# Retention products rebuilt around whole pairs of heads; the second norm's transposes kept on the chip; loads of the second and third tile group issued piece by piece into new homes

## The chip, the cores and the metric

One core of one Trainium2 chip runs the kernel. The metric is device microseconds, the median of the timed runs. Engines are named as the profile names them: PE (TensorE), DVE (VectorE), ACT (ScalarE), POOL (GpSimd), SP (the queue of loads and stores).

## The reference

One layer over 1024 prompt tokens and 8 x 16 sample tokens, 1152 in all (nine tiles of 128 tokens: `t` 0 to 7 are the prompt, tile 8, called `ST`, the samples). All in float32.

```
h = rms_norm(x, norm1_g); z = h @ w_in            # 8 retention heads, 8 fox heads, 64 wide each
retention per chunk: sc = (q k^T) * decay mask
                     o  = sc v + (q S) * q_dec;   S = S * s_dec + (k * k_dec)^T v
forgetting attention per head (softmax over all earlier tokens, cumulative log-forget bias)
x1 = x + concat(norm(ro) * silu(rg), norm(fo)) @ w_out
PEER: xn = rms_norm(x1, norm2_g); scores of 2 x 8 x 128 keys, top 16 of 16 x 16 pairs per head,
      act = gelu(sum(xn * u[e])); y = x1 + sum(g * act * v[e])        # 128 experts e per token
```

For each token PEER fetches 128 rows of 2048 numbers (`u` and `v` of one expert side by side), so a tile of 128 tokens needs 128 gathers of 128 rows of 8 KB.

## The kernel before, in words

Four phases follow one another: norm, projections of the retention keys and values, `phase_retention`, the fox projections of the first three tiles, and then `phase_tail`, which is most of the time.

**Retention.** Tiles are taken in `ORDER` = 0, 1, ST, 2, ..., 7. In one iteration PE makes the scores of the next tile (`scores`, in two halves: even heads at partitions 0 to 63, odd heads at 64 to 127), the eight gate products of this tile (`gate(t, k)`, 128x512 each, spread between the others), and the outputs: per head one product of the masked scores with the values (L683) and one of the queries with the state (L686, on 64 partitions). `up` (L694) is the update of the state. DVE masks scores, updates the state, and forms the gated output; for four tiles PE and DVE also make a piece of the sample tiles' state (L732). `outputs_sample` (L706, L710) is the sample tile, whose products over 64 rows are only 16 columns wide. `WARM` adds two bf16 products ahead of each gate run.

**Tail.** Nine tiles in three groups of three (`g`). Per gather POOL issues an indirect DMA into a ring of nine buffers; DVE makes the dot product of the fetched `u` with the token's `xn`, spread over partitions (`xrep`); for each four gathers ACT and DVE form weights, and PE adds the `v` halves into `yp` (`add_v`, eight products of 128x512, four at a time on 32 columns each), after which the buffers are free (`uv_free`) and POOL goes on. `replicate_x` and `spread_x` make `xrep` of the next tile near a tile's end; `finish` closes a tile. Everything else of a group (fox attention, `w_out`, second norm, keys, top-k: the "front") is dealt between these steps: `front_steps` lists the steps with what each waits for, and `deal` puts them at fixed places of each engine's program by estimated durations. An engine runs its program strictly in order. Gathers of a tile need that tile's experts, so the first three tiles' gathers follow the front of group 0, and the fronts of groups 1 and 2 run beside gathers.

The transposed `xn` of each tile is stored to the scratch `xts` (L1539) and loaded back one tile ahead (L1557) for `replicate_x`; `x1` is stored too (L1528) and loaded for the sum in `finish` (L1577).

Of the kernel before, what the change touches and what calls it, by code (L numbers as in the profile page):

```python
# [12 lines left out]
ALU = mybir.AluOpType  # L13
# [3 lines left out]
P = 128  # L17
# [15 lines left out]
def emit(nc, a):  # L33

    ctx = ExitStack()
    with ctx:
# [555 lines left out]
        def phase_retention(block, sem, ps):  # L592
# [15 lines left out]
            op_all = [ps(f"op{i}", [P, GW]) for i in range(2)]  # L608
            op = [b[:, 0:PAIRS * HD].rearrange("p (r e) -> p r e", r=PAIRS) for b in op_all]
# [12 lines left out]
            pool_step, gate_exp = sem("pool_step"), sem("gate_exp")  # L622
# [37 lines left out]
            def _(pe):  # L660
                def scores(t, half):
                    s = AT[t]
                    if s >= 1:
                        pe.wait_ge(mask_done, 2 * (s - 1) + half + 1)
                    for r in range(PAIRS):
                        b0 = 64 * half
                        last = nc.tensor.matmul(sc[half][:, r, :], kT[b0:b0 + 64, r, t * P:(t + 1) * P],
                                                qT[b0:b0 + 64, r, t * P:(t + 1) * P], start=True, stop=True)
                    last.then_inc(sc_done, 1)

                def outputs(t):
                    s = AT[t]
                    if t >= 1:
                        pe.wait_ge(oev, t)
                        pe.wait_ge(st_done, t)
                    if t == 2:
                        pe.wait_ge(oTm, 1)
                    for h in range(NH):
                        if h < 2:
                            pe.wait_ge(mask_done, 2 * s + h + 1)  # L680
                        b0, r = 64 * (h % 2), h // 2
                        o = op[h % 2][:, r, :]
                        last = nc.tensor.matmul(o, sT[:, s % 2, h % 2, r, :], vn[:, t, h * HD:(h + 1) * HD],  # L683
                                                start=True, stop=(t == 0))
# [3 lines left out]
                        if h == NH - 1:  # L688
                            last.then_inc(o_done, 1)
                        if s and h % 2:  # L690
                            gate(t, 2 + h // 2)
                    for h in range(NH):
# [7 lines left out]
                def outputs_sample():  # L700
# [3 lines left out]
                    for h in range(NH):  # L704
# [9 lines left out]
                        if h in (0, 1, 2, 4, 5, 6):  # L714
                            gate(ST, h + (1 if h < 3 else 0))
# [1772 lines left out]
```

## Time and profile before

| | |
|---|---|
| time, median of 3 runs | 3847.42 us (3836.97 to 3848.2) |
| the profiled execution's own time | 3865.37 us |
| its span | 3863.6 us |
| busy: PE, DVE, POOL, ACT | 2370.1, 2448.0, 1428.5, 473.8 us |
| moved by DMA in the span | 1357.89 MB, of them 1208.03 MB by gathers |
| retention begins, fox projections begin, first gather issued | 226, 427, 692 us |

The rows below come from that one execution, so sums are made against 3865.37 us. It is 17.95 us above the median of the three runs. Each float32 product of the code shows as two MATMUL records on PE.

### The profile page before, as it was taken

What the parts mean: (1) busy time and instruction counts of PE and PEld (TensorE: products, weight loads), DVE (VectorE), ACT (ScalarE), POOL (GpSimd) and SP (SyncE); (2) the same over time, 40 slices, a digit from 0 to 9 for tenths busy, and PEclk for the clock granted to TensorE, in tenths of its full rate; (3) what the DMA queues carried; (4) which work ended last, traced back from release to release, by engine and by line L of the source; (5) the groups of instructions that cost most, each with busy time, mean ns of one, the idle gap of its engine ahead of it and who ended that gap; (6) DMA issues with size and microseconds to landing.
All of it is one profiled execution on the core that took longest, in us unless ns stands there. A gap on an engine that the chain in (4) does not pass through costs nothing.

```text
span 3863.6 us, 34930 instructions
## 1 busy us (share of the span) xinstructions
PE 2370.1 (61%) x11957; PEld 970.8 (25%) x11957; DVE 2448.0 (63%) x6334; ACT 473.8 (12%) x1311; POOL 1428.5 (37%) x1275
## 2 busy tenths in 40 slices
PE   8999989778477566846547655684343334334333
PEld 4455445323133122314213311231010001001000
DVE  4225324989566556878966655788886555555555
ACT  2001132202022010102112200110111000000000
POOL 1001100265344443433444444434444444444443
PEclk9988999989688787967668877897666556566655
DMA  3010451899999999999999999999999999999998
GB/s 117 22 39 17 130 191 55 334 395 406 411 410 415 420 418 394 409 391 404 415 417 420 409 420 418 409 407 416 409 407 422 421 420 417 413 422 410 421 421 366
DMA packets 251073, 1357.89 MB, mean 351 GB/s; under 512 B 33792, under 2 KB 53064, under 8 KB 103440
## 3 DMA queue, kind: packets, MB, share of 16 engines
q0 software_dynamic: 165888, 1208.03, 75.8%
q1 hardware_dynamic: 84720, 147.04, 10.5%
q8 instruction: 95, 1.56, 0.2%
q14 instruction: 82, 0.67, 0.0%
q10 hardware_dynamic: 288, 0.59, 0.0%
HBM read 1325.22 MB, written 30.35 MB: 351 GB/s over the span
## 4 chain that ended last, share of the span: by engine, by line
DMA 36%; PE 20%; DVE 16%; POOL 8%; issue 6%; ACT 1%; another core or an unknown queue 0%; POOLq 0%; DVEq 0%; ACTq 0%
DMA M<-in_peer_uv,M 36%; PE yp L2067 12%; POOL M L1632 8%; DVE M L2352 6%; PE ab L2020 1%; PE ef L2055 1%; DVE exg L2369 1%; DVE strips L2374 1%; PE ab L1861 1%; PE c L1999 1%; PE d L1883 1%; DVE M L2119 1%; PE d L1999 1%; DVE gel L2361 1%; DVE M L2118 1%
## 5 line engine op out<-in xcount | busy, mean ns | idle before, releaser
L1632 POOL DMA_INDIRECT M<-in_peer_uv,M x1152 | 1321.8, 1147 | 1801.5 <-PE yp L2067 1445.0
L2352 DVE SCALAR_TENSOR_TENSOR M<-M 128x1024 f32<-128x1024 f32 x1152 | 1411.0, 1226 | 856.5 <-DMA M<-in_peer_uv,M 824.5
L2067 PE MATMUL yp<-M,strips 128*32 128x512 f32 x4608 | 898.5, 921 | 1279.4 <-DVE strips L2374 1253.8
L2067 PEld LDWEIGHTS yp<-M,strips 128*32 128x32 f32 x4608 | 159.2, 144 | 1888.4 <-DVE strips L2374 1490.5
L1813 ACT ACTIVATE gel<-gel 128x4 f32<-128x4 f32 x288 | 59.2, 205 | 2151.8 <-DVE gel L2363 2117.5
L2020 PE MATMUL ab<-M 128*128 128x512 f32 x576 | 264.9, 608 | 1.3 <-ACT M L1769 1.3
L426 PE MATMUL z<-M 128*128 128x512 f32 x432 | 190.1, 597 | 0.9 <-PEq L105 0.9
L2020 PEld LDWEIGHTS ab<-M 128*128 128x128 f32 x576 | 108.2, 196 | 137.6 <-issue 136.1
L1900 PE MATMUL ab<-M 128*128 128x512 f32 x288 | 130.6, 605 | 5.2 <-DVEq L2229 5.2
L867 POOL TENSOR_SCALAR small<-small 128x8 f32<-128x8 f32 x9 | 2.6, 285 | 331.7 <-DVE small L837 331.7
L426 PEld LDWEIGHTS z<-M 128*128 128x128 f32 x432 | 81.3, 191 | 97.5 <-issue 97.4
L2374 DVE SCALAR_TENSOR_TENSOR strips<-gel,exg 128x128 f32<-128x128 f32 x288 | 84.0, 292 | 32.9 <-ACT gel L1813 22.5
L2352 DVE DVE_READ_ACCUMULATOR M<-M 128x1 f32 x1152 | 95.0, 83 | 0.0
L2055 PE MATMUL ef<-ident,M 128*32 128x128 f32 x2304 | 86.7, 290 | 13.2 <-issue 11.9
L1873 PE MATMUL c<-ident,M 128*128 128x128 f32 x288 | 56.1, 308 | 61.1 <-ACT M L1666 60.4
L2246 DVE CUSTOM_DVE_ANT_0 M<-ab,M 128x896 f32<-128x896 f32 (+6 forms) x64 | 48.4, 756 | 70.6 <-PE ab L1862 59.3
L747 PE MATMUL z<-M 128*128 128x512 f32 x144 | 91.9, 738 | 0.8 <-DMA M<-in_w_in 0.8
L1861 PE MATMUL ab<-M 64*128 64x512 f32 (+3 forms) x192 | 87.9, 568 | 5.1 <-DVE mins L2246 5.1
L2369 DVE TENSOR_TENSOR exg<-e,gel 128x128 f32<-128x128 f32 x288 | 84.0, 292 | 10.0
L1883 PE MATMUL d<-M 128*64 128x128 f32 x576 | 89.1, 308 | 0.9 <-ACT M L1674 0.9
L2055 PEld LDWEIGHTS ef<-ident,M 128*32 128x32 f32 x2304 | 69.1, 117 | 39.1 <-issue 29.3
L1883 PEld LDWEIGHTS d<-M 128*64 128x64 f32 x576 | 72.5, 156 | 18.0 <-issue 16.2
(248 smaller groups left out, 2517.6 us busy)
## 6 DMA issues: line engine op xcount, KB each, us to landing
M<-in_peer_wq SPq DMA_DIRECT2D x12, 2048.0 KB, 28.5
M<-in_w_in SPq DMA_DIRECT2D x9, 2048.0 KB, 11.3
M<-in_peer_uv,M POOLq DMA_INDIRECT x1152
M<-in_w_out SPq DMA_DIRECT2D x24, 512.0 KB, 23.4
M<-in_x_prompt SPq DMA_DIRECT2D x16, 512.0 KB, 10.9
x_scratch<-M SPq DMA_DIRECT2D x9, 512.0 KB
xts_scratch<-M SPq DMA_DIRECT2D x9, 512.0 KB
M<-xts_scratch SPq DMA_DIRECT2D x9, 512.0 KB
```

What stands on the lines that cost most here:

```text
L426: last = nc.tensor.matmul(z[n % 3][:, :], hT[:, k, t * P:(t + 1) * P], wbuf[:, slot(gi), k, :], start=(k == 0), stop=(k == KC - 1))
L747: last = nc.tensor.matmul(z[s % 2][:, :], hT[:, k, t * P:(t + 1) * P], w_gate[k], start=(k == 0), stop=(k == KC - 1))
L1632: nc.gpsimd.indirect_dma_start(ring[n % NR], None, a["peer_uv"], bass.IndirectOffsetOnAxis(ap=idxH[:, t % 6, s // 4, s % 4:s % 4 + 1], axis=0)
L1861: nc.tensor.matmul(s[:, c:c + w], rows_q[b0:b0 + 64, r], rows_k[b0:b0 + 64, r, c:c + w], start=True, stop=c + w < width)
L1883: last = nc.tensor.matmul(Dk[b0:b0 + 64, 0:P], (vg if g else vn)[:, j, h * HD:(h + 1) * HD], pT[:, n % 2, j, :], start=(j == 0), stop=(j = ...
L1900: last = nc.tensor.matmul(half_ab[j % 2], hTl[i][:, k, :], pw[q % 2][:, k, :], start=(k == 0), stop=(k == KC - 1))
L2020: last = nc.tensor.matmul(half_ab[i % 2], xT[:, tt, k, :], wq(g, b)[:, k, :], start=(k == 0), stop=(k == KC - 1))
L2055: last = nc.tensor.matmul(EF[32 * b:32 * b + 32, half, k * P:(k + 1) * P], xTn[:, 4 * half + k, 32 * j:32 * j + 32], ident[:, :], start=Tr ...
L2067: last = nc.tensor.matmul(yp[32 * j:32 * j + 32, 512 * c:512 * c + 512], strips[:, n % 2, j, :], ring[(4 * n + j) % NR][:, D + 512 * c:D + ...
L2352: nc.vector.scalar_tensor_tensor(out=row, in0=row, scalar=1.0, in1=xrep[:, s % 4, :], op0=ALU.mult, op1=ALU.mult, accum_out=dots[:, t % 2, ...
L2369: link(nc.vector.tensor_tensor(exg[:, :, :], bc(e32[:, :].unsqueeze(1), [P, 4, 32]), bc(g[:, 3, :].unsqueeze(2), [P, 4, 32]), ALU.mult))
L2374: nc.vector.scalar_tensor_tensor(out=strips[:, n % 2], in0=bc(g[:, 2, :].unsqueeze(2), [P, 4, 32]), scalar=1.0, in1=exg[:, :, :], op0=ALU. ...
```

## The change

**Retention.** `scores` alternates the two halves head by head. The state is also written as a block-diagonal matrix `bd` (two heads per 128x128 block, zeroed once by POOL, its two diagonal parts written by two more DVE instructions per tile), and the eight state products on 64 partitions become four on 128, after the eight score products of the tile. The outputs of all heads lie in one bank per tile, and ACT moves them in one copy instead of two. Gate products 0 and 1 follow each other, and those of the sample tile all come after its outputs.

**Tail.** The scratch `xts` is gone: no store, no load. `x1` is loaded once per tile into the buffer that held the transposes (`load_x1`, `x1b`), DVE makes the normalised row again (`make_row`), PE spreads it by identity products, and PE adds `x1` into `yp` by eight identity products at the start of a tile, so `finish` is a copy. The loads of groups 1 and 2 are cut up: keys (`loadk`), the rest of the attention's data (`load`), `w_out` half by half (`wload`, `hload`), query weights (`qload`, `rload`) and keys, each issued when its new home is free. Planner costs change with them.

```diff
+                def scores(t):
                     for r in range(PAIRS):
+                        for half in range(2):
+                            b0 = 64 * half
+                            last = nc.tensor.matmul(sc[half][:, r, :], kT[b0:b0 + 64, r, t * P:(t + 1) * P],
+                                                    qT[b0:b0 + 64, r, t * P:(t + 1) * P], start=True, stop=True)
...
-                        if t:
-                            last = nc.tensor.matmul(o, qT[b0:b0 + 64, r, t * P:(t + 1) * P],
-                                                    st[b0:b0 + 64, r, :], start=False, stop=True)
...
+                        for r in range(PAIRS):
+                            last = nc.tensor.matmul(o[:, r * P:(r + 1) * P], qT[:, r, t * P:(t + 1) * P], bd[:, r, :],
+                                                    start=False, stop=(r == PAIRS - 1))
...
-                        if h in (0, 1, 2, 4, 5, 6):
-                            gate(ST, h + (1 if h < 3 else 0))
...
+                    whole = s == 0 or t == ST
...
+                    for b0 in (0, 64):
+                        nc.vector.tensor_tensor(bd[b0:b0 + 64, :, b0:b0 + 64], new[b0:b0 + 64], sd[b0:b0 + 64], ALU.mult)
+                    nc.vector.tensor_tensor(st, new, sd, ALU.mult).then_inc(st_done, 1)
...
-                add(rest, ("load", g), sp=(55.0 if g else 6.0, *routed))
                 if g:
-                    add(rest, ("loadq", g), sp=(40.0, *chosen))
+                    at = routed if nt < GT else [("sp", ("pturn", 0, 2 * LATE - 1)), ("pe", ("pmm", 0, 2 * LATE - 1, 1))]
+                    add(rest, ("loadk", g), sp=(25.0, *at))
+                add(rest, ("load", g), sp=(40.0 if g else 6.0, *routed))
...
-                        sp.dma_start(a["xts"][t], xT[:, arg[0]].rearrange("p k n -> p (k n)")).then_inc(xT_out, 16)
...
+                def load_x1(t):
+                    sp.wait_ge(x1_out, 16 * GT * (t // GT + 1))
+                    if t >= 1:
+                        sp.wait_ge(x1b_used, t)
+                    sp.dma_start(x1b, a["x1"][t]).then_inc(x1b_in, 16)
...
-                        for k in range(4):
-                            for b in range(4):
-                                last = nc.tensor.matmul(EF[32 * b:32 * b + 32, half, k * P:(k + 1) * P],
-                                                        xTn[:, 4 * half + k, 32 * j:32 * j + 32], ident[:, :],
-                                                        start=True, stop=True)
+                        for b in range(4):
+                            last = nc.tensor.matmul(EF[32 * b:32 * b + 32, half, :], ident[:, 32 * j:32 * j + 32],
+                                                    xb[:, 512 * half:512 * half + 512], start=True, stop=True)
...
+                    if k == 0:
+                        pe.wait_ge(x1b_in, 16 * (t + 1))
+                        for c in range(2):
+                            for j in range(4):
+                                last = nc.tensor.matmul(yp[32 * j:32 * j + 32, 512 * c:512 * c + 512], ident[:, 32 * j:32 * j + 32],
+                                                        x1b[:, 512 * c:512 * c + 512], start=True, stop=False)
+                        last.then_inc(x1b_used, 1)
...
-                    nc.vector.tensor_tensor(xb, yp[:, :], xb, ALU.add).then_inc(y_out, 1)
+                    if t + 1 < TILES:
+                        dve.wait_ge(rep_mm, 8 * t + 16)
+                    else:
+                        dve.wait_ge(out_done, 16 * t)
+                    nc.vector.tensor_copy(xb, yp[:, :]).then_inc(y_out, 1)
+
+                def make_row(t):
+                    dve.wait_ge(x1b_in, 16 * (t + 1))
+                    dve.wait_ge(xrs, t + 1)
+                    if t >= 2:
+                        dve.wait_ge(out_done, 16 * (t - 1))
+                    nc.vector.scalar_tensor_tensor(out=xb, in0=x1b, scalar=rst[:, t:t + 1], in1=grow[:, :],
+                                                   op0=ALU.mult, op1=ALU.mult).then_inc(row_done, 1)
```

PE before, in retention, the iteration of tile 1 from its start (`sc` scores, `z` gate, `op` outputs of two heads):

```order
L667 MATMUL sc_3<-M 128x128 x4
L745 MATMUL z_3<-identb 128x512 x2
L747 MATMUL z_3<-M 128x512
L667 MATMUL sc_3<-M 128x128 x4
L747 MATMUL z_3<-M 128x512
L683 MATMUL op_3<-M 128x64
L686 MATMUL op_3<-M 128x64
L683 MATMUL op_3<-M 128x64
L686 MATMUL op_3<-M 128x64
L747 MATMUL z_3<-M 128x512
```

The same place of the changed kernel, up to the end of the tile's outputs:

```order
L668 MATMUL sc_3<-M 128x128 x8
L747 MATMUL z_3<-identb 128x512 x2
L749 MATMUL z_3<-M 128x512 x2
L681 MATMUL op_3<-M 128x64 x2
L749 MATMUL z_3<-M 128x512
L681 MATMUL op_3<-M 128x64 x2
...
L749 MATMUL z_3<-M 128x512
L691 MATMUL op_3<-M 128x128 x4
L698 MATMUL up<-M 64x64 x8
```

The scores stand together, the alternation of L683 and L686 is gone, and four wide products (L691) follow the last head.

PE before, from the scores ahead of the sample tile to the first of its eight heads (`opT`) and the gate product behind it:

```order
L667 MATMUL sc_3<-M 128x128 x8
L745 MATMUL z_3<-identb 128x512 x2
L747 MATMUL z_3<-M 128x512
L706 MATMUL opT<-M 64x128
L710 MATMUL opT<-M 64x16 x8
L747 MATMUL z_3<-M 128x512
```

The end of the sample tile in the changed kernel, and the start of the next iteration:

```order
L710 MATMUL opT<-M 64x128
L714 MATMUL opT<-M 64x16 x8
L747 MATMUL z_3<-identb 128x512 x2
L749 MATMUL z_3<-M 128x512 x8
L723 MATMUL up<-ident,M 128x128 x4
L668 MATMUL sc_3<-M 128x128 x8
```

All eight gate products of the sample tile now stand in a row behind its narrow products.

DVE of the changed kernel in the top-k work ahead of the first gather (L2200 and L2208 are the choice of experts of tile 0; before, nothing stood between L2127 and L2169, which are L2158 and L2200 here):

```order
L2154 MAX M<-M 128x8 x4
L2158 MAX_INDEX M<-M 128x8 x4
L2424 SCALAR_TENSOR_TENSOR M<-M,dec 128x1024
L2200 MAX_INDEX M<-M 128x8 x4
L2208 CAST M<-M 128x64
```

`make_row(0)` (L2424) has moved in between, and PE's `replicate_x` of tile 0 waits for it.

## Rows read from the trace of the kernel before

**Rows 1.** The page: mean busy share of the DMA engines, in 40 equal slices, tenths.

```profile
DMA  3010451899999999999999999999999999999998
```

**Rows 2.** Windows by phase: length, busy us (instructions) of each engine, granted clock, DMA share, GB/s.

```profile
226.00:427.00 201.00, 198.63 (x886) 114.97 (x887) 91.87 (x112) 18.85 (x40) 17.48 (x19) 0.83 0.15 44
427.00:692.00 265.00, 243.48 (x1068) 123.99 (x1068) 96.59 (x345) 69.61 (x173) 21.30 (x28) 0.97 0.36 124
692.00:3864.00 3172.00, 1721.82 (x9431) 632.71 (x9429) 2193.40 (x5768) 353.96 (x1045) 1380.03 (x1206) 0.73 1.00 411
```

**Rows 3.** Waits: us in total, times, longest us.

```profile
POOL M L1632 <- ACT M L1680: 76.3, 3, 75.7
```

**Rows 4.** DMA from 692 us on: packets; issues with KB each.

```profile
DMA packets 209074, 1302.72 MB, mean 411 GB/s; under 512 B 21024, under 2 KB 29280, under 8 KB 61472
...
M<-xts_scratch SPq DMA_DIRECT2D x7, 512.0 KB
...
xts_scratch<-M SPq DMA_DIRECT2D x6, 512.0 KB
```

**Rows 5.** Timeline of PE, tile 4 of retention: start, us, what, records.

```profile
343.73 1.16 PE L667 MATMUL sc<-M 64*128 64x128 f32 x8
...
348.26 0.33 PE L683 MATMUL op<-M 128*128 128x64 f32 x2
348.52 0.43 PE L686 MATMUL op<-M 64*128 64x64 f32 x2
...
349.61 1.13 PE L747 MATMUL z<-M 128*128 128x512 f32 x2
...
357.60 0.69 PE L694 MATMUL up<-M 128*64 128x64 f32 x16
...
361.33 1.16 PE L667 MATMUL sc<-M 64*128 64x128 f32 x8
```

**Rows 6.** Timeline of PE, runs of one kind: tile 0's outputs, a projection.

```profile
231.07 3.67 PE L683 MATMUL op<-M 128*128 128x64 f32 x16
...
448.98 7.03 PE L426 MATMUL z<-M 128*128 128x512 f32 x16
```

**Rows 7.** Timeline of PE, sample tile and tile 2.

```profile
263.07 1.71 PE L667 MATMUL sc<-M 64*128 64x128 f32 x16
...
266.46 1.10 PE L710 MATMUL opT<-M 64*64 64x16 f32 x16
...
272.57 1.89 PE L710 MATMUL opT<-M 64*64 64x16 f32 x16
...
297.44 2.07 PE L667 MATMUL sc<-M 64*128 64x128 f32 x8
...
326.13 1.16 PE L667 MATMUL sc<-M 64*128 64x128 f32 x8
```

**Rows 8.** Windows of 10 us in retention, columns as in Rows 2.

```profile
230.00:240.00 10.00, 9.19 (x43) 6.78 (x41) 2.49 (x4) 1.28 (x3) 1.84 (x2) 0.50 0.95 240
240.00:250.00 10.00, 10.00 (x32) 4.84 (x31) 2.56 (x2) 0.60 (x1) 0.00 (x0) 0.87 0.02 3
```

**Rows 9.** Timeline of DVE, tile 4 of retention: first and last of 13 rows.

```profile
358.33 0.42 DVE L814 TENSOR_TENSOR M<-up,M 128x256 f32<-128x256 f32 x1 [4.19 <-PE up L694]
...
370.45 1.29 DVE L804 TENSOR_TENSOR M<-sc,causal 128x512 f32<-128x512 f32 x2 [0.21 <-DVE M L846]
```

**Rows 10.** Timeline of PE and POOL ahead of the first gather.

```profile
657.40 7.32 PE L2055 MATMUL ef<-ident,M 128*32 128x128 f32 x256
...
713.09 0.94 POOL L1632 DMA_INDIRECT M<-in_peer_uv,M  x1 [9.28 <-PE yp L2067]
```

**Rows 11.** Timeline at the end of tile 7.

```profile
3535.13 1.90 PE L2067 MATMUL yp<-M,strips 128*32 128x512 f32 x16
...
3539.27 0.34 SPq L1571 DMA_DIRECT2D out_y_prompt<-M  x1
...
3541.76 3.64 PE L2067 MATMUL yp<-M,strips 128*32 128x512 f32 x16 [4.73 <-DVE strips L2374]
```

More of the change, by code:

```diff
@@ L750, in gate @@
                         last.then_inc(z_done, 1)
-                for half in range(2):
-                    scores(0, half)
+                scores(0)
                 for s, t in enumerate(ORDER):
-                    for half in range(2):
-                        if s + 1 < TILES:
-                            scores(ORDER[s + 1], half)
-                        if t == ST:
-                            if half:
-                                gate(t, 0)
-                        elif s:
-                            gate(t, half)
+                    whole = s == 0 or t == ST
+                    if s + 1 < TILES:
+                        scores(ORDER[s + 1])
+                    if not whole:
+                        gate(t, 0)
+                        gate(t, 1)
                     if t == ST:
@@ L768, in _ @@
                         state_sample(PIECE[t])
-                    for k in range(KC - 1 if s else 0, KC):
+                    for k in range(0 if whole else KC - 1, KC):
                         gate(t, k)
@@ L863, in _ @@
             def _(pool):
+                nc.gpsimd.memset(bd[:, :, :], 0.0).then_inc(bd_set, 1)
                 for s in range(TILES):
@@ L880, in _ @@
                         act.wait_ge(o_done, t + 1)
-                        for par in range(2):
-                            last = nc.scalar.copy(
-                                mixo[:, t, 0:GW].rearrange("p (r q e) -> p q r e", q=2, e=HD)[:, par], op[par])
-                        last.then_inc(oev, 1)
+                        nc.scalar.copy(mixo[:, t, 0:GW], op[t % 2][:, :]).then_inc(oev, 1)
                         act.wait_ge(oev, t + 1)
@@ L906, in emit @@
         NR = 9
+        ROW = P - 20
         def tiles_of(g):
@@ L996, in values @@
                 t, nt = FOX[n][2], len(tiles_of(g))
+                wait = [("sp", ("load", g))] if g and n == FIRST[g] else []
                 add(rest, ("foxv", g, n),
-                    pe=(0.1 + 0.33 * (t + 1), ("act", ("foxq" if t >= 4 else "foxp", g, n)),
+                    pe=(0.1 + 0.33 * (t + 1), ("act", ("foxq" if t >= 4 else "foxp", g, n)), *wait,
                         *bank("D", "act", ("foxv", g, n))),
@@ L1044, in front_steps @@
                 full = ("dve", ("fout", g, PAIRS - 1))
-                add(rest, ("hload", g), sp=(50.0 if g else 12.0, full))
+                add(rest, ("hload", g), sp=(30.0 if g else 12.0, full))
                 for i in range(GT):
@@ L1189, in work_ready @@
                 if e == "dve":
+                    if i % P == ROW and i // P + 1 < TILES and ("sp", ("hadd", (i // P + 1) // GT, GT - 1)) not in done:
+                        return None
                     return None if i >= len(landed) or summing() else landed[i]
@@ L2393, in _ @@
                             finish(t - 1)
+                        if s == ROW and t + 1 < TILES:
+                            make_row(t + 1)
                 for step in due["dve"][P * TILES]:
```

196 lines of the change are left out of this document (106 added, 90 removed).

## Prediction

> **What bounds the kernel now.** I read the windows by phase first. From 692 us on, the DMA engines' share is 1.00 and they move 411 GB/s [rows 2]; the page's DMA line reads 9 in every slice from the ninth on, with an 8 in the last alone [rows 1]. So the last 3172 us are as long as the bytes take: 1302.72 MB [rows 4] at 411 GB/s are 3170 us. The waits say the same from the other side. POOL waited for a tile's experts 76.3 us in three waits, of which 75.7 us are the one before the first gather [rows 3]: the fronts of groups 1 and 2 held up no gather, and the tail is not short of experts, it is short of bandwidth. An earlier front gains nothing there.
>
> Ahead of 692 us it is the other way round. In retention, 226 to 427 us, PE is busy 198.63 of 201 us, at a mean granted clock of 0.83, with DVE at 91.87 us and DMA at 0.15; in the fox projections and the front of group 0, PE has 243.48 of 265 us at clock 0.97 [rows 2]. What PE saves in retention therefore moves everything behind it forward, the first gather too, and nothing later gives it back, since the tail's length is a number of bytes.
>
> **Retention, one tile at full clock.** Tile 4's iteration runs from 343.73 to 361.33 us, 17.6 us [rows 5]. Two heads' outputs, eight records in which L683 (128 rows) and L686 (64 rows) alternate, take from 348.26 to 349.61, 1.35 us, so a tile has 4 x 1.35 = 5.4 us, 0.169 us a record. Where L683 stood alone, in tile 0, 16 records took 3.67 us [rows 6] in a stretch whose granted clock was 0.50, which is 1.2 GHz [rows 8]; at 2.4 GHz that is 0.115 us a record. After the change a tile has 16 records of the scores' products and 8 of the four block-diagonal ones, all on 128 rows: 24 x 0.115 = 2.75 us, 2.65 less. If the alternation were not what costs, 24 x 0.169 = 4.05, 1.35 less; I take the first, since L683 is the same instruction in both rows.
>
> The Trainium skill says in "TensorEngine Tiling (Array Packing)", Key Properties, that changing the tiling mode drains the engine. That is a reason for the gap between 0.115 and 0.169, which the rows show on their own.
>
> Scores: two runs of 8 records take 1.16 us each [rows 5]; where 16 stood together they took 1.71 us [rows 7], 0.6 less. The new order alternates upper and lower halves of the array. No row has that; the nearest is `up`, which alternates halves of columns, 16 records in 0.69 us [rows 5]. Full overlap would halve 1.71, 0.85 more. Between 0.6 and 1.45 I take 0.9 us a tile.
>
> So 3.5 us go and 14.1 us are left. DVE's work for tile 4 runs from 358.33 to 371.74 us, 13.4 us with its waits [rows 9]. Two writes of `bd` are added, each of 256 elements a partition on 64 partitions: at most 0.42 us by the state's row, and at least half of that, if only the partitions' number counted. 13.4 + 0.84 = 14.25 us, so DVE is now as long as PE: had the scores saved all 1.45 us, DVE would keep the half of it. POOL's one memset and ACT's single copy lie beside PE's first scores.
>
> **Retention, the clock.** In the sample tile the granted clock fell: the same 16 narrow records take 1.10 us at 266.46 and 1.89 us at 272.57 [rows 7]. It stayed at 1.2 GHz, with gates spread between narrow products, into tile 3: scores of 8 records take 2.07 us at 297.44 and 1.16 us at 326.13. So the sample tile took 34.4 us (263.07 to 297.44) and tile 2 28.7 us (297.44 to 326.13). The change puts the sample tile's eight gate products in a row. The trace has such a place: tile 0, where eight gates followed narrow products at clock 0.50 and the clock was back within the next window, which reads 0.87 [rows 8]. A row of eight is 7.03 us at full clock [rows 6]. I expect: scores 1.7; 3 us of narrow products at full clock; the other 8 us at the half, x 1.72 = 14; warm-up 0.9; three gates at half clock and five at full, 6 + 4.3; transposes 0.5: 30.4 us, 4 less. Tile 2 then runs at full clock and needs 14.1, less about 1 for the piece of state that it has not (L732, two products of 512 columns): 13 us, 15.7 less.
>
> Sum for retention: start 0.5, tile 1 3.5, sample tile 4.0, tile 2 15.7, tiles 3 to 6 4 x 3.5 = 14, tile 7 (no scores behind it) 2.65: **40.4 us less**. Bounds: tile 2 still at half clock, 28.5; clock never down, 50.
>
> **Ahead of the first gather.** `make_row(0)` stands on DVE in the top-k chain that ends in the first gather, +1.2 us (an operation of 128x1024). PE's `replicate_x(0)`, 657.40 to 664.72 us before [rows 10], must wait for it, some 6 us. Behind it stand query products and the first `add_v`, which freed buffers at 713.09 us; nine gathers of 1.05 MB are 23 us of DMA work from 692 on, and 2 MB of weights join them, so this lateness is covered. Without cover it would cost 6 us once.
>
> **The tail.** From 692 us on, seven loads and six stores of `xts`, 0.524 MB each, go [rows 4]; the other three stores and two loads lay before. 13 x 0.524 = 6.82 MB at 411 GB/s: **16.6 us less**. All other bytes stay, in other pieces. There is no cover over this: the queue is full.
>
> The Trainium skill's "DMA: Bandwidth & Descriptors", Specifications, gives about 358 GB/s of HBM per core. By it the same bytes would be worth 19.0 us, but this trace moves 411 GB/s, so the measurement decides.
>
> At the eight tile starts PE gets 16 more records on `yp`, as one `add_v`: 1.90 us at full clock, 3.64 at the half. They can run between the release of `yp`, 3539.27 us, and the next `add_v`, 3541.76, 2.5 us in which PE waited for DVE [rows 11]. So 0 to 1.2 us are late each time, and behind them the buffers, with several gathers still queued. I take 2 us in all; bounds 0 and 10. `make_row` and the copy in `finish` cost DVE 1.2 us a tile where it has 2193 busy of 3172 us [rows 2]; the replication's 8 products a piece on 512 columns are as many columns as before.
>
> Sum: -40.4 + 1.2 - 16.6 + 2 = **-53.8 us**. Against the profiled execution that is 3865.4 - 53.8 = 3811.6 us; it lies 17.95 above the median, so on the median 3847.4 - 53.8 = **3793.6 us**.
>
> **Rivals.** (A) as above. (B) The clock stays at 1.2 GHz through tile 2 as it did before: retention gives 28.5, the time is 3805.5. For it: the narrow products now stand together, twice as long without a wide one between. Against: tile 0's recovery. (C) The clock does not fall at all, or the scores overlap wholly: 3784. For it speaks only `up`. (D) Retention gives less than half, because DVE's chain or the outputs' single bank makes PE wait: some 15 us, which leaves 3819 to 3831. Against: DVE's 14.25 us beside 14.1. (E) Slower: loads of groups 1 and 2 now have shorter allowances (30 for 50 in `hload`), PE reaches a product whose weights are in flight, `add_v` stands behind it in PE's order, POOL gets no buffer and the queue runs dry. It must cost over 54 us, over twelve large loads more than 4.5 us of dry queue each. Against: while PE waits for a load, DMA is moving that load, so only the latency behind it is lost; and there is no wait on experts now. 3860. (F) The stores and loads removed were hidden: then DMA's share would be below 1.00 somewhere. It isn't; 3810, inside the range.
>
> **Chances.** A 0.50, B 0.23 (F 0.03 with it), C 0.13, D 0.08, E 0.03. A measurement of this kernel tells some 0.3%, 11.5 us, from no change. A, B, C, F and nearly all of D are faster by more than that, 0.93; within it 0.04, the edge of D with part of E; slower 0.03. The range goes from C with a little recovered queue time, 3771, to B with all bounds of the tile starts, 3805.5 + 8 and some noise, 3818.
>
> **What would show it.** Right: retention's length 201 us down to about 161; tile 4's iteration 14.1; granted clock near 0.9 there; first gather near 653 us; the stretch from first gather to end some 3157 us, at 411 GB/s. Wrong: a low clock in tile 2 (B); DVE rows in retention that PE waits for (D); a DMA share under 1.00 in windows where PE waits on weights (E).

## The result, and the profile after

The changed kernel takes **3821.15 us**, the median of 13 runs (3816.67 to 3829.06); the kernel before, run beside it, 3848.2 us (13 runs, 3836.97 to 3874.74). The ratio is 0.9924, 95% interval 0.9906 to 0.9942: faster by 27 us, where 53.8 were forecast. The forecast of 3793.6 us is 27.6 us too low, and its range ended 3 us short. Of the executions behind the medians below, two took about twice the time, 7481.31 us (x1_only) and 8249.65 us (after_again), and are left out.

The profiled execution took 3816.67 us, 48.7 us less than the profiled one of before. Already here two things part: between the two profiled executions the forecast misses by 5 us, between the two medians by 27.

Windows by phase of the kernel after (columns as in [rows 2]):

```profile
226.00:374.00 148.00, 146.34 (x836) 85.66 (x832) 98.03 (x128) 18.20 (x31) 18.29 (x20) 0.92 0.22 60
374.00:640.00 266.00, 237.50 (x842) 114.69 (x842) 97.42 (x343) 68.68 (x171) 20.94 (x28) 0.96 0.33 113
640.00:3815.00 3175.00, 1736.59 (x8068) 595.94 (x8066) 2201.02 (x5778) 355.42 (x1047) 1362.15 (x1206) 0.72 1.00 408
```

Retention is 148 us long where it was 201 [rows 2], the middle phase as long as it was, and the tail 3175 us where it was 3172. The first gather starts at 640.46 us and not at 692: the stages ahead of it gave 51.6 us, more than forecast. The tail gave nothing, though it moves fewer bytes. Its DMA traffic, from 640 us on:

```profile
DMA packets 207207, 1295.73 MB, mean 408 GB/s; under 512 B 20832, under 2 KB 29088, under 8 KB 59616
```

That is 6.99 MB less than [rows 4] and at 408 GB/s, not 411. 1295.73 MB at 411 GB/s are 3153 us, so against the rate of before some 22 us were lost to a queue that ran empty, and the share still reads 1.00: the mean of 3175 us is too coarse for it. In windows of 10 us it is plain (same columns):

```profile
845.00:855.00 10.00, 0.00 (x0) 0.00 (x0) 2.21 (x6) 1.11 (x3) 1.41 (x2) 0.69 0.67 266
855.00:865.00 10.00, 9.28 (x33) 3.52 (x34) 9.58 (x34) 1.27 (x3) 5.83 (x5) 0.80 0.41 134
...
1370.00:1380.00 10.00, 9.42 (x35) 4.73 (x36) 6.48 (x25) 0.59 (x1) 0.80 (x1) 0.78 0.11 44
...
1615.00:1625.00 10.00, 5.76 (x36) 2.56 (x40) 5.89 (x20) 1.18 (x3) 0.40 (x1) 0.57 0.58 220
2205.00:2215.00 10.00, 6.74 (x27) 3.09 (x28) 3.90 (x15) 0.59 (x1) 0.82 (x1) 0.54 0.67 273
```

**The chain behind one of them.** Timeline of the kernel after around 1370 us, of SP, PE and POOL in turn (in brackets the idle time before, and what ended it):

```profile
1312.44 4.24 SPq L1408 DMA_DIRECT2D M<-in_peer_wq  x2
1327.38 13.46 SPq L1568 DMA_DIRECT2D M<-in_keys_t  x2
...
1347.73 3.31 PE L2098 MATMUL yp<-M,strips 128*32 128x512 f32 x16 [9.24 <-DVE strips L2407]
1370.58 2.04 PE L2064 MATMUL d<-M 128*128 128x128 f32 x8 [19.54 <-issue]
1372.42 4.63 PE L2046 MATMUL ab<-M 128*128 128x512 f32 x8
1376.98 1.92 PE L2098 MATMUL yp<-M,strips 128*32 128x512 f32 x16
...
1355.42 0.95 POOL L1656 DMA_INDIRECT M<-in_peer_uv,M  x1 [0.30 <-issue]
1379.20 0.95 POOL L1656 DMA_INDIRECT M<-in_peer_uv,M  x1 [22.83 <-PE yp L2098]
```

L2064 is the first product with the second group's keys, and by the program its wait is on `key_in`: the slowest of the keys' four loads in this execution landed 43.1 us after its issue, and 1327.38 + 43.1 is 1370.5. The keys, two loads of 256 KB, were issued from 1327.38 on, behind two loads of weights of 2 MB each; the planner allowed 32 us from the transposes to them. PE stood 19.54 us before it with `add_v` (L2098) behind it in its program, so POOL got no buffer for 22.83 us, and the gathers it had issued by 1355.42 were all moved by 1370. How such loads fare beside the gathers, from 1312 to 1371 us (queue, packets, MB, share of 16 engines; issues with KB each and median us to landing):

```profile
q0 software_dynamic: 2614, 19.03, 77.8%
q1 hardware_dynamic: 2502, 5.23, 23.3%
...
M<-in_peer_wq SPq DMA_DIRECT2D x2, 2048.0 KB, 42.4
...
M<-in_keys_t SPq DMA_DIRECT2D x2, 256.0 KB, 39.3
```

SP's queue moved 5.23 MB in 59 us while the gathers moved 19.03, so a quarter of a megabyte behind 4 MB takes as long as 2 MB. The Trainium skill says in "DMA: Bandwidth & Descriptors", Queues, rings and completion order, that every queue is served in turns on the same engines, packet by packet, and that within one the descriptors are consumed in order. These rows agree: the two queues moved 2502 and 2614 packets, so SP's had its turns, but of smaller packets.

The other three are of the same kind. Waits of the kernel after from the first gather on (columns as in [rows 3]):

```profile
PE d L2064 <- issue: 40.4, 2, 20.8
...
PE yp L2092 <- DVE M L2417: 27.1, 6, 5.9
...
PE ab L1963 <- DMA M<-in_cache_fox_k: 20.9, 1, 20.9
...
ACT M L1728 <- DMA qts_scratch<-M: 20.0, 1, 20.0
```

L2064 waited a second time, up to 2208 us, for the third group's keys (`issue` in its row again stands for that load). L1963 waited for the sample's cached keys, where it had waited 6.9 us before. At 851 us ACT's copy of a late projection stood 20.0 us for the store out of the same buffer, issued at 819.78 us behind a 2 MB load of `w_in`, and the running tile's gelu stood behind it; the planner has that store done after 6 us. The row of L2092, x1's products at the tile starts, comes up below.

**Retention.** Timeline of PE in the kernel after, tile 4, and scores of the sample tile, tile 2 and tile 3:

```profile
255.47 1.16 PE L668 MATMUL sc<-M 64*128 64x128 f32 x16
...
273.00 8.22 PE L749 MATMUL z<-M 128*128 128x512 f32 x16
...
281.59 1.16 PE L668 MATMUL sc<-M 64*128 64x128 f32 x16
...
293.58 1.16 PE L668 MATMUL sc<-M 64*128 64x128 f32 x16
...
306.77 1.16 PE L668 MATMUL sc<-M 64*128 64x128 f32 x16
...
310.02 0.56 PE L681 MATMUL op<-M 128*128 128x64 f32 x4
310.41 1.08 PE L749 MATMUL z<-M 128*128 128x512 f32 x2
...
315.24 1.05 PE L691 MATMUL op<-M 128*128 128x128 f32 x8
316.23 0.69 PE L698 MATMUL up<-M 128*64 128x64 f32 x16
...
319.96 1.16 PE L668 MATMUL sc<-M 64*128 64x128 f32 x16
```

A tile's iteration is 13.2 us (306.77 to 319.96), not the 14.1 forecast. The 16 records of scores take 1.16 us; in [rows 7] 16 took 1.71 in one run, in [rows 5] 2 x 1.16. The outputs came out close to the forecast. Counted from start to start, as the 5.4 us of before were, they take 4 x 0.39 (310.02 to 310.41) + 0.99 (315.24 to 316.23) = 2.55 us for 24 records, where 2.75 was forecast. The sample tile took 26.1 us (forecast 30.4) and tile 2 12.0 (forecast 13), after the run of gates at 273.00.

### The profile page after: what moved, and what is told of

It is laid out like the page before. It is cut to its first block, busy times and chain, and to the rows that moved or that the text cites. A ratio compares the mean times of both kernels' runs of the same rounds, so it can differ in the third digit from the quotient of the medians.

```text
span 3814.9 us, 31668 instructions
## 1 busy us (share of the span) xinstructions
PE 2326.4 (61%) x10317; PEld 895.6 (23%) x10317; DVE 2462.7 (65%) x6359; ACT 473.9 (12%) x1303; POOL 1411.4 (37%) x1276
## 4 chain that ended last, share of the span: by engine, by line
DMA 37%; PE 20%; DVE 16%; POOL 8%; issue 6%; ACT 1%; SPq 0%; POOLq 0%; DVEq 0%; ACTq 0%
DMA M<-in_peer_uv,M 33%; PE yp L2098 11%; POOL M L1656 7%; DVE M L2385 7%; DMA M<-qts_scratch 2%; PE ab L2046 2%; PE ab L1885 1%; DVE exg L2402 1%; DMA M<-in_cache_fox_k 1%; DVE strips L2407 1%; PE d L2025 1%; PE c L2025 1%; PE d L1909 1%; DMA qts_scratch<-M 1%; DVE M L2150 1%
## 5 line engine op out<-in xcount | busy, mean ns | idle before, releaser
L2098 PE MATMUL yp<-M,strips 128*32 128x512 f32 x4608 | 887.4, 911 | 1203.3 <-DVE strips L2407 1203.2
L2098 PEld LDWEIGHTS yp<-M,strips 128*32 128x32 f32 x4608 | 157.7, 144 | 1820.5 <-DVE strips L2407 1480.8
L426 PE MATMUL z<-M 128*128 128x512 f32 x432 | 188.4, 593 | 0.9 <-PEq L105 0.9
L2080 PE MATMUL ef<-M,ident 128*32 128x512 f32 x576 | 78.2, 682 | 8.6 <-DVE M L2424 7.0
L2064 PE MATMUL d<-M 128*128 128x128 f32 x288 | 44.8, 303 | 61.2 <-issue 40.4
L749 PE MATMUL z<-M 128*128 128x512 f32 x144 | 75.0, 631 | 0.1
L2025 PE MATMUL c<-M 128*128 128x512 f32 x144 | 72.7, 653 | 3.7 <-ACT M L1781 3.5
```

Of the source, the lines that this page charges most:

```text
L426: last = nc.tensor.matmul(z[n % 3][:, :], hT[:, k, t * P:(t + 1) * P], wbuf[:, slot(gi), k, :], start=(k == 0), stop=(k == KC - 1))
L2025: last = nc.tensor.matmul((C, Dk)[c][:, :], mT[:, t % 2, k, :], wout(g, k)[:, 512 * c:512 * c + 512], start=(k == 0), stop=(k == KC - 1))
L2080: last = nc.tensor.matmul(EF[32 * b:32 * b + 32, half, :], ident[:, 32 * j:32 * j + 32], xb[:, 512 * half:512 * half + 512], start=True, s ...
L2098: last = nc.tensor.matmul(yp[32 * j:32 * j + 32, 512 * c:512 * c + 512], strips[:, n % 2, j, :], ring[(4 * n + j) % NR][:, D + 512 * c:D + ...
```

## Experiments

The experiments ran on several chips, so each kernel stands beside the kernel before on its own chip. That yardstick is a coarse one: the medians of before run from 3847.16 to 3870.73 us and its executions from 3836.97 to 3884.53, while the changed kernel gave 3821.15 on one chip and 3823.45 on another. Medians in us; "gather" is the start of the first gather in the profiled execution, "tail" the span less that:

| kernel | median | before there | gather | tail |
|---|---|---|---|---|
| before (profiled) | 3848.2 | | 692.09 | 3171.5 |
| after | 3821.15 | 3848.2 | 640.46 | 3174.4 |
| ret_only | 3818.57 | 3854.28 | 643.62 | 3173.7 |
| tail_only | 3854.34 | 3854.28 | 668.51 | 3169.7 |
| x1_only | 3852.19 | 3854.28 | 703.28 | 3167.3 |
| ret_x1 | 3811.11 | 3854.28 | 641.49 | 3166.7 |
| keys_late | 3815.77 | 3847.16 | 642.03 | 3166.7 |
| waits_priced | 3796.54 | 3847.16 | 642.43 | 3148.8 |
| after_again | 3823.45 | 3870.73 | 641.66 | 3173.4 |
| stores_priced | 3815.2 | 3870.73 | 641.52 | 3167.1 |
| bytes_back | 3812.1 | 3870.73 | 647.81 | 3169.2 |
| waits_priced_2 | 3794.18 | 3870.73 | 640.21 | 3147.1 |

A tail is that of one execution, and a difference of a few us between two of them proves nothing by itself: the kernel before had 3171.5 and, once more (before_look, below), 3178.6 us, and the tail of the changed kernel, left as it is in gates_spread, gs_a and gs_b below, took 3175.7, 3173.2 and 3165.8 us.

### The parts of the change one by one

**ret_only**: the kernel before and the part of the diff inside `phase_retention`.

> The kernel before with the rebuilt retention stage alone; the tail is that of before, its transposes stored and its loads where they stood. Theory (the gain is retention's, the tail's is lost to its own waits): first gather near 640.5 us, from there to the end 3171.5 us as before, so 3848 - 52 = 3796 us, 25 us under the changed kernel's 3821. Rival (the 52 us are not retention's rebuild alone, since the tail's edits shift when its first loads are due): first gather later than 645 us and a time over 3803 us.

3818.57 us, 0.9889 of before (0.9832 to 0.9946). First gather (643.62) and tail are within some 3 us of the theory, but the time is 22.6 us over it. The theory's own two parts, 640.5 and 3171.5, add up to 3812 and not to 3796: the 52 us came off an execution that was long, and were then taken from a median. The kernel before has a median of 3854.28 here, with a first gather at 692 in the profile that I subtracted from and, as the next three show, often earlier. Between medians retention alone gives 35.7 us, no less than the whole change.

**tail_only**: the reverse, the diff without its part in `phase_retention`.

> The changed kernel with the retention stage of before put back; the tail has both of its edits (no stored transposes, loads moved). Theory (some 16 us fewer bytes, some 20 us more of empty ring, and a little more): first gather at 692 us, from there to the end 3174 us, in all 3848 + 3 = 3851 us. Rival (the tail's loss comes from its meeting the rebuilt retention, for instance from another phase between the gathers and the planned loads): the predicted tail, 3157 us, and 3834 us in all.

3854.34 us, ratio 0.9987 (0.9957 to 1.0016). The tail edits together are worth nothing that can be measured, with the old retention too; the rival falls. The profile holds more. The old stage ended at 400.81 us, 26.7 us sooner than in the profile of before, with the same instructions. Timeline of PE in tail_only, scores of the sample tile, tile 2 and tile 3:

```profile
261.02 1.71 PE L667 MATMUL sc<-M 64*128 64x128 f32 x16
283.04 1.16 PE L667 MATMUL sc<-M 64*128 64x128 f32 x8
...
299.44 0.82 PE L667 MATMUL sc<-M 64*128 64x128 f32 x5
```

The sample tile took 22.0 us, not 34.4, and tile 2 16.4, not 28.7 [rows 7]: here the granted clock read 1.00 in every window of 5 us from 240 to 335, so it never left 2.4 GHz. The old stage without a fall took 174.5 us and the rebuilt one without a fall 145.7 (gs_a, below): 28.8 us are the products' own gain.

**x1_only**: before, with no transposes stored; DVE's row and PE's x1 in their place. Homes and loads stay.

```diff
-                        sp.dma_start(a["xts"][t], xT[:, arg[0]].rearrange("p k n -> p (k n)")).then_inc(xT_out, 16)
...
-                    sp.dma_start(xTn.rearrange("p k n -> p (k n)"), a["xts"][t]).then_inc(xTn_in, 16)
+                    sp.dma_start(x1b, a["x1"][t]).then_inc(x1b_in, 16)
```

> The kernel before with one edit of the tail alone: transposes neither stored nor reloaded, the row made by DVE from x1, x1 added by PE. The loads, their homes and their planned costs stay as before, as does retention. Theory (removed bytes are worth their time while no new wait for a load stands against them): 13 transfers of 0.524 MB less, -16.6 us, +2 for the tile starts, 3848 - 14 = 3834 us, first gather at 693 us. Rival (the bytes are worth nothing, their time was hidden or is taken up by the row and by the new start of each tile's sum): 3847 to 3851 us.

3852.19 us, 0.9983 (0.9954 to 1.0013), just over the rival's 3847 to 3851. In the profile the tail is 4.2 us shorter than in the profile of before, no more than two tails of one kernel can differ. The first gather is late, at 703.28 us, though retention took 182.5 us only: the front of group 0 ran at half clock. Windows of x1_only (columns as in [rows 2]):

```profile
480.00:520.00 40.00, 37.92 (x119) 18.02 (x120) 5.86 (x26) 13.55 (x44) 0.00 (x0) 0.59 0.58 197
520.00:560.00 40.00, 39.30 (x117) 19.45 (x117) 5.95 (x26) 12.79 (x44) 0.00 (x0) 0.50 0.25 79
```

**ret_x1**: both of these edits.

> Both edits that the theory holds for gains, without the third: the rebuilt retention and the transposes not stored; loads, homes and planned costs of the second and third group as before. Theory: 3848 - 52 - 14 = 3782 us, 39 us under the changed kernel. Rival (the bytes are worth nothing): 3796 us, as with retention alone. Rival (the moved loads are innocent, the ring runs empty because tiles now start without the stored transposes): 3796 us or more, and the waits of PE for keys and weights near 1330 and 2200 us appear here too.

3811.11 us, 0.9873 (0.9815 to 0.9931). That is 7.5 us under ret_only (tails 7.0 apart) and 10 under the changed kernel. The four executions of each do not overlap (3807.29 to 3815.26, 3815.43 to 3819.53). So removing the stored transposes gives 7, not the 16.6 of its bytes, and moving the loads seems to cost 8 to 10 (tails 7.7 apart), though that is a comparison of two chips. With the rest of the 16.6 go two empty stretches that ret_only does not have, at 850 us (again a store of `qts_scratch`, 19.7 us) and at 1750 (ret_only has a smaller one of its own, a share of 0.53 from 1460 to 1470 us). There POOL waited for the indices of tile 3, whose routing was chosen too late; waits of ret_x1, 1690 to 1775 us, columns as in [rows 3]:

```profile
POOL M L1631 <- PE yp L2071: 36.3, 5, 9.1
POOL M L1631 <- ACT M L1679: 23.4, 3, 22.8
```

x1_only has both as well, 19.6 us for the store and 21.5 us of POOL up to 1828 us. The keys' waits of after are not here, so those belong to the moved loads, as the second rival denied; but that rival is right in that the first edit opens waits of its own.

### Waits cured by their price

**keys_late**: one number of the planner, the allowance from a group's last transpose to its keys.

```diff
-                        sp=(32.0 if g and i == GT - 1 else 6.0, ("act", ("hxt", g, i))))
+                        sp=(60.0 if g and i == GT - 1 else 6.0, ("act", ("hxt", g, i))))
```

> The changed kernel with one number of the planner changed: the step that loads the second and third group's first two key blocks is due 60 us after its transposes are ready for whoever needs the keys, not 32. Theory (PE's score step stood ahead of keys still in flight and held the sums of the running tile behind it, 19.5 us idle at 1350 and 20.8 at 2195 us): both waits gone, the ring never runs empty there, and of the 10.3 + 5.4 us lost at those two places most comes back: 3821 - 13 = 3808 us. Rival (the lost time of the tail is set by the whole of what the engines must do in it, and a wait that goes comes back elsewhere): those waits go and others grow, 3817 to 3825 us.

3815.77 us: 5.4 under the changed kernel on another chip, by its ratio to before (0.9908, 0.9881 to 0.9936) about the same, and not clear of the interval. The waits at 1350 and 2195 us are gone, the tail is 7.7 us shorter, half of what was expected. The waits behind the stretches at 850 and 1620 us stayed (19.9 and 21.9 us), and POOL had a new one at 1780. Between theory and rival.

**waits_priced**: the other two prices as well (the stores of `pact` from 6 to 26 too).

```diff
-                    add(rest, ("sload", g), sp=(45.0, *routed))
+                    add(rest, ("sload", g), sp=(65.0, *routed))
...
-                            add(rest, ("pnrm", 0, m), dve=(1.3, ("pool", ("ppow", 0, m)), *old), sp=(6.0, ("dve", ("pnrm", 0, m))))
+                            add(rest, ("pnrm", 0, m), dve=(1.3, ("pool", ("ppow", 0, m)), *old), sp=(26.0, ("dve", ("pnrm", 0, m))))
...
-                            act=(0.7, ("pe", ("pturn", 0, m)), *old), sp=(6.0, ("act", ("pturn", 0, m))))
+                            act=(0.7, ("pe", ("pturn", 0, m)), *old), sp=(26.0, ("act", ("pturn", 0, m))))
```

> As the kernel with the late keys, and the other steps whose transfers were late are priced as they measured too: stores of the late projections 26 us instead of 6, the loads ahead of the sample tile's attention 65 instead of 45. Theory: the empty stretches at 850 us (9.4 us) and 1620 us (5.7 us) go as well: 3808 - 12 = 3796 us. Rival: a later plan makes a group's routing late for its first tile, POOL waits for indices at a tile's start, and the time is 3817 us or more.

3796.54 us, 0.9859 (0.9802 to 0.9916), what the theory gave. The four stretches that were empty are full. waits_priced_2, the same kernel on the chip of the next two:

```profile
855.00:865.00 10.00, 9.51 (x38) 3.87 (x36) 9.65 (x14) 1.09 (x2) 5.76 (x5) 1.00 1.03 415
...
1370.00:1380.00 10.00, 5.02 (x24) 1.40 (x21) 4.95 (x12) 1.17 (x4) 1.97 (x2) 0.71 1.02 417
...
1615.00:1625.00 10.00, 4.39 (x24) 1.54 (x24) 9.76 (x30) 1.12 (x3) 1.61 (x2) 0.83 1.02 421
2205.00:2215.00 10.00, 6.89 (x21) 2.15 (x22) 6.52 (x14) 0.20 (x1) 3.43 (x3) 0.66 1.02 425
```

**after_again** and **waits_priced_2** put the two beside each other on one chip.

> The changed kernel itself, on the same chip as the next three, so that they are compared with it and not with times of another chip. Expected by all theories: 3817 to 3829 us, first gather within 3 us of 640.5 us, the empty stretches at 850, 1370, 1620 and 2210 us again.

> The kernel with all three prices once more, beside the changed kernel on one chip. Theory: 24 us under the changed kernel, 3797 us. Rival (the first run's 24.6 us were partly the difference of two chips): less than 15 us under it.

3823.45 against 3794.18 us: 29 us apart, tails 26.3, and no execution of the one (3816.88 to 3823.62) near one of the other (3789.12 to 3797.44). A version with five numbers of the planner changed beats both kernels.

**stores_priced**: as waits_priced, the keys at 32 again.

> The changed kernel with the late projections' stores priced 26 us and the sample tile's loads 65 us; the keys stay at 32. It takes the three prices apart. Theory (each price cures its own empty stretch and they add up: keys alone gave 5.4 us, all three together 24.6): the stretches at 850 and 1620 us go, those at 1370 and 2210 us stay, 3821 - 15 = 3806 us, at most 3802. Rival (the gain of all three comes from one plan that happened to fit, not from cured waits): 3815 us or more, or under 3797 us with the keys' waits still there.

3815.2 us, 8.2 under the changed kernel beside it; the tail is 6.3 us shorter, not 15. The stretches at 850 and 1620 us went, and the keys' two waits stayed, 16.1 and 18.7 us. The second still emptied the queue (share 0.24 from 2260 to 2270 us), and a stretch came up that was full in after, 0.40 from 2140 to 2150, where POOL waited for ACT. Timelines of PE and POOL in stores_priced:

```profile
2259.64 2.05 PE L2064 MATMUL d<-M 128*128 128x128 f32 x8 [18.71 <-issue]
...
2144.56 1.05 POOL L1620 TENSOR_SCALAR dec<-small 128x1 f32<-128x1 f32 x1 [14.05 <-ACT M L1787]
```

So the gains do not add up: 5.4 and 8.2 alone, 29 together. While one kind of load was still priced too low, curing another opened a new empty stretch, here at 2140 us and in keys_late at 1780. That the keys' price and the other two together give far more than either alone is shown. The other two (the stores' and the sample's) were never changed apart, and since every price also moves the rest of the plan, part of the 29 us may be the plan's own luck; that is not separated.

**bytes_back**: waits_priced, with 12 transfers given back.

```diff
+                        sp.dma_start(a["xts"][t], xT[:, arg[0]].rearrange("p k n -> p (k n)")).then_inc(xT_out, 16)
+                        if t >= GT:
+                            sp.dma_start(a["xtt"][t], xT[:, arg[0]].rearrange("p k n -> p (k n)")).then_inc(xT_out, 16)
```

> The kernel with all three prices, and 12 transfers of 0.524 MB given back to the tail: each tile's transposes of the second and third group are stored, twice (the first group's once, before the gathers); nobody reads them. Theory (once no wait empties the ring, a byte in the tail costs its time at 411 GB/s, as the prediction took it for the changed kernel): 12 x 1.28 = 15.3 us more, 3797 + 15 = 3812 us. Rival (transfers of this size find room beside the gathers, the removed bytes were worth little): 3797 to 3802 us.

3812.1 us, 17.9 over waits_priced_2 where 15.3 was expected. The tail's traffic, of waits_priced_2 and of bytes_back:

```profile
DMA packets 207207, 1295.73 MB, mean 412 GB/s; under 512 B 20832, under 2 KB 29088, under 8 KB 59616
```

```profile
DMA packets 208935, 1302.02 MB, mean 411 GB/s; under 512 B 21024, under 2 KB 29280, under 8 KB 61344
```

6.29 MB more at about the same rate. The two tails are 22.1 us apart, more than the 17.9 of the medians, so the price of 15.3 is the low end of what was measured. The edit also puts the first group's stores ahead of the gathers, and in this profile retention was 3.5 us longer than in most; both are outside the tail, but inside the medians. In a tail whose queue stays full a byte costs at least its time; the price in the forecast was about right, its condition was not met.

### The clock in the old stage

**before_look**: the kernel before, once more.

> The kernel before, unchanged, looked at once more. Theory (the length of the old retention stage differs from execution to execution with where the granted clock falls: first gather was seen at 692.1 us, and with the same retention in two experiments at 668.5 and 703.3): first gather between 668 and 703 us, the rest 3171 us after it, the total between 3837 and 3880 us. Rival (the stage is steady at 692 us, and the runs differ in the tail): first gather within 2 us of 692.1 us.

First gather at 677.39 us: theory. The tail is 3178.6 us, 7 more than the theory's 3171. Together with the stage in tail_only and x1_only, the old retention took 200.9 us (226.57 to 427.5), 182.6, 174.5 and 182.5. Windows over the stage, in tail_only and in the changed kernel run again:

```profile
226.00:401.00 175.00, 173.17 (x894) 101.18 (x895) 91.83 (x113) 18.68 (x39) 17.99 (x19) 0.97 0.17 51
```

```profile
226.00:375.00 149.00, 146.59 (x834) 85.74 (x834) 98.03 (x128) 18.20 (x31) 18.56 (x20) 0.92 0.21 60
```

The execution the forecast started from was the longest of the four, by 18.4 us over the two in the middle, about what it lay above the median (17.95). The rebuilt stage took 148.2 to 149.2 us in eight executions of nine (152.6 in the ninth, bytes_back), at clock 0.92.

**gates_spread, gs_a, gs_b**: the changed kernel with the sample tile's gates between its heads as before, three executions.

```diff
+                        if h in (0, 1, 2, 4, 5, 6):
+                            gate(ST, h + (1 if h < 3 else 0))
...
-                    whole = s == 0 or t == ST
+                    whole = s == 0
```

> The changed kernel with the sample tile's eight gate products spread between its heads again, as before, all else of the rebuilt retention kept. Theory of the prediction (the long run of gate products behind the heads brings the full clock back before tile 2): the clock stays at half through tile 2, its iteration takes 20 us and more instead of 12.0, first gather at 651 to 656 us instead of 640.5. Rival (whether the clock falls here is chance from execution to execution, and where the gates stand does nothing): the sample tile takes 26 us or, with no fall, 22, tile 2 takes 12, and the first gather comes at 637 to 643 us.

> The changed kernel with the sample tile's gates between its heads, looked at a second time. Theory (where the gates stand sets how long the granted clock stays at half: behind the heads it was low for 14 us in seven executions of nine, and for 16 and 22 in the others): low for 17 us or more, retention 152 us or longer. Rival (chance alone): low for anything from 0 to 14 us, retention 149 us or shorter.

> The changed kernel with the sample tile's gates between its heads a third time. Theory: half clock for 17 us or more, retention 152 us or longer. Rival (chance alone): 0 to 14 us, retention 149 us or shorter.

Retention 151.9, 145.7 and 151.9 us (226.57 to 378.5, 225.49 to 371.18, 228.70 to 380.57); first gather at 645.33, 636.85 and 674.66 us, the last with the front of group 0 at half clock as in x1_only. In two the clock was low for 17 us, from 270 to 287 and from 272 to 289 us, where in the changed kernel it was low for 14, from 262 to 275; in gs_a it never fell. Windows over gs_a's stage:

```profile
226.00:371.00 145.00, 139.67 (x832) 78.09 (x829) 98.04 (x128) 18.18 (x31) 18.12 (x19) 0.98 0.23 62
```

Neither side wins: with spread gates the stage had a fall in two executions of three, with grouped ones in each of nine, and the return came sooner. What the forecast expected of spread gates, tile 2 at half clock, did not come: tile 2 took 13.1 us in gates_spread.

**og_a, og_b**: the old stage with its sample gates in one run, two executions.

> The kernel before with one edit in its old retention stage: the sample tile's eight gate products stand in one run behind its heads, as in the changed kernel. All else is as before. The old stage was at half clock for 57, 19, 0 and 17 us in four executions, and took 200.9, 182.6, 174.5 and 182.5 us. Theory (the place of the gates makes the stage steady): low for 10 to 16 us, the stage 180 to 184 us, in both looks. Rival (the rest of the rebuild makes it steady, or chance): the two looks differ by more than 5 us, or one is low for over 20 us or for none.

> The old retention stage with its sample tile's gates in one run, a second time, with the same expectations as the first look: theory 180 to 184 us in both; rival over 5 us between them, or half clock for over 20 us or for none.

182.3 and 180.9 us (225.99 to 408.3, 226.74 to 407.62), clock 0.93 and 0.92 over the stage. Both lengths are in the theory's range, the clock was low for some 17 us where 10 to 16 were expected. But two executions are few, and the old stage as it stood took 182.5 and 182.6 us in two of four. That grouping keeps the 200.9 away is likely, and not shown.

## Why the prediction was wrong

**The tail term failed.** "There is no cover over this: the queue is full", read from a share of 1.00 over 3172 us and a row of nines. The price of the bytes was about right (bytes_back: 17.9 us for 12 transfers, 15.3 forecast), and a tail of 3157 us was possible: waits_priced has 3147 to 3149. But the changed kernel has 3174.4, since its queue ran empty at four places. The queue was not even full before. Against rival F the prediction says of a share below 1.00 "It isn't"; the kernel before had such a place (columns as in [rows 2]):

```profile
1510.00:1520.00 10.00, 10.00 (x37) 4.29 (x36) 9.59 (x42) 0.79 (x2) 4.51 (x4) 0.88 0.51 183
```

The 411 GB/s therefore were a mean with a gap in it, which left waits_priced room to come out 8 to 10 us under 3157. What I missed is in two sentences. "The fronts of groups 1 and 2 held up no gather" was true of before and said nothing of how little was to spare: without the stored transposes alone, tile 3's indices came 22.8 us late. And I left the shifted allowances without a price (the term of rival E, put at nothing in the sum).

**Rival E's mechanism came, at a small size.** The argument against it, "while PE waits for a load, DMA is moving that load, so only the latency behind it is lost", was half true. In the 59 us up to 1371 the engines moved 411 GB/s. But PE waits 20 us and frees no buffer in them, the gathers issued by 1355.42 last until 1370, and the next one is issued at 1379.20, behind PE's next `add_v`: 9 to 10 us of empty queue at 1370 us, half of PE's wait. I asked that each of twelve loads cost over 4.5 us. Four places cost some 22 us together at the rate of before (1295.73 MB: 3174.4 us less 3153), and 26 to 27 against the same bytes in waits_priced_2 (3147.1); either is all of the 16.6 and more. E's chance of 0.03 was for a slower kernel; the same mechanism as a deduction from A had no chance at all.

**The stage ahead of the gathers: right in kind, under-sized in the profile, over-counted on the median.** In the profile retention gave 52.4 us, not 40.4. An iteration lost 4.4 us and not 3.5: the scores gave 1.1 a tile where 0.9 was taken, the outputs 2.85 where 2.65 was, and the gates, with two of them side by side, 0.5 where nothing was; the sample tile gave 8.3, not 4, and tile 2 16.7, not 15.7. DVE did not become the bound (D falls). But the forecast was moved to the median by a constant 17.95 us. The profiled execution was above the median for a reason, the half clock in the sample tile and tile 2, and 19.7 of the 40.4 us (4.0 and 15.7) were that clock coming back. The median execution did not have them to give: between medians retention gives 35.7 us, and from the usual 182.5 us of the old stage to 148.5 it is 34. With that and the tail's 2.9 us, the sum is 3848.2 - 35.7 + 2.9 = 3815.4 us; 3821.15 was measured. The last 6 us, which carry the time out of the range, stay open. The 35.7 come from another chip, whose median of before is 6.1 us higher (3854.28), while ret_only and the changed kernel are only 2.6 us apart, so they may be no more than the scatter of before.

**make_row(0), +1.2 us**, ahead of the first gather: the middle phase is 266 us against 265, no more than that. **Tile starts, +2 us**: PE waited there for DVE's copy of `yp` (L2092 on L2417), 27.1 us at six starts, 4.5 each and far over the 1.2 assumed, and 38.0 us at seven in waits_priced_2. Yet that kernel's tail is the shortest of all, so these waits can cost it little: the queued gathers cover them. The 2 us were not measured by themselves.

**Rival B** (tile 2 at half clock throughout) came in no execution of the new stage; with spread gates only its first 2 to 3 us were at half clock. **C** (clock never down) was seen once in twelve, with the gates spread.

## What to carry to other kernels

A mean DMA share of 1.00 says that the queue is full on average, not that it has slack against a late load: look at windows of some 10 us, in the kernel before too, and at what each in-order engine has behind a wait for a load. Price loads in a plan by their landing beside the other traffic, the small ones behind large ones like the large ones; in this kernel wrong prices hid one another, and mending them together gave more than one by one. And before a profile's gain is carried over to a median, ask which part of it belongs to that execution alone: the time that a fallen clock would give back is no gain where it does not fall.

## What the runs showed that I had not expected

- Beside gathers that fill the DMA engines, 256 KB loads issued 10 us behind two of 2 MB landed after 39.3 us (median), the 2 MB ones after 42.4; SP's queue got 5.23 of 24.27 MB in 59 us.
- Products that alternate between the upper and lower 64 rows of the array, record by record, took 1.16 us for 16; in two runs by halves 1.71 (261.02 in tail_only), both at full clock.
- The same instruction stream took from 174.5 to 200.9 us in one stage, by where the granted clock fell to 1.2 GHz and how long it stayed; and the front of group 0 could fall as well (0.59 and 0.50 in x1_only, 0.71 to 0.50 in gs_b), some 28 us at the first gather, in two executions of eighteen.
